# A two-layer encoder on one core: attention's weighted sum in plain float32 with two column halves of the array, in place of split operands

## The reference

```
proj = rms_norm(x) @ w_in            # latents (A), q/k/v of 6 heads (B), q/k/v of 4 heads (C)
o_a = dense attention, 6 heads       # q and k have 64 + 32 rotary features, v has 64
o_b = dilated sliding attention, 6 heads of 64
o_c = neighbourhood attention on a 16 x 64 grid, 4 heads of 64, with a bias
x = x + concat(norm(o_a), norm(o_b), norm(o_c)) @ w_out
x = x + square(relu(rms_norm(x) @ w_mlp_in)) @ w_mlp_out
```

```
p = softmax(scores)                  # scores: queries x keys
o = p @ v                            # the weighted sum: v has 64 columns per head
```

## Time and profile before

| quantity | value |
|---|---|
| median of three runs | 2985.09 us |
| span of the profiled execution | 2983.4 us |
| TensorE matmul busy | 2876.5 us (96%) |
| VectorE busy | 1733.5 us (58%) |
| ScalarE busy | 1081.0 us (36%) |
| mean granted TensorE clock | 0.983 |
| attention, layer 1 and layer 2 | about 292 to 665 us and about 1762 to 2145 us |

### The profile page before, as it was taken

How to read it: one execution, slowest core, us unless ns; L and a number is a source line. 1 busy time by engine, 2 the same in 40 slices (tenths; PEclk the granted TensorE clock), 3 DMA queues, 4 the chain that set the end, 5 groups by cost and what they waited for, 6 DMA issues and landing times.

```text
span 2983.4 us, 43794 instructions
## 1 busy us (share of the span) xinstructions
PE 2876.5 (96%) x14640; PEld 2454.8 (82%) x14640; DVE 1733.5 (58%) x3038; ACT 1081.0 (36%) x2056; POOL 26.5 (1%) x53
## 2 busy tenths in 40 slices
PE   7999999979999999999999999999799999999998
PEld 7998888867888888888799988887688888888886
DVE  5642778865555455455656337788655555455457
ACT  5332768864311111111334236777632111111113
POOL 0000000000000000000000000000000000000000
PEclk9999999989999999999999999999799999999999
DMA  5657534463111111111146573336530111111111
GB/s 192 185 179 181 123 84 94 103 160 120 43 43 56 42 42 56 42 56 49 59 166 200 168 182 88 87 93 142 133 108 29 56 42 56 42 43 55 42 61 69
DMA packets 194043, 281.45 MB, mean 94 GB/s; under 512 B 47184, under 2 KB 153296, under 8 KB 184144
## 3 DMA queue, kind: packets, MB, share of 16 engines
q1 hardware_dynamic: 190032, 262.56, 30.5%
q0 software_dynamic: 3840, 16.78, 1.5%
HBM read 208.50 MB, written 70.78 MB: 94 GB/s over the span
## 4 chain that ended last, share of the span: by engine, by line
PE 83%; DVE 5%; issue 5%; DMA 4%; ACT 2%; DVEq 1%; ACTq 0%; SPq 0%; POOLq 0%
PE ps L1349 23%; PE ps L1174 19%; PE ps L1364 17%; PE ps L1247 7%; PE ps L1264 6%; PE ps L1293 6%; DMA biasC<-in_bias_c 2%; PE ps L1304 2%; PE ps L1211 1%; PE ps L1142 1%; DVE hn L841 1%; DVE x L1095 1%; DMA values<-vst 1%; DVE vbuf L1082 1%; ACT rbuf L774 1%
## 5 line engine op out<-in xcount | busy, mean ns | idle before, releaser
L1364 PE MATMUL ps<-w_dn,hid 128*128 128x512 f32 x3072 | 713.1, 391 | 1.4
L1349 PE MATMUL ps<-hT,w_up 128*128 128x512 f32 x3072 | 702.6, 389 | 3.1 <-DVE hT L824 3.1
L1364 PEld LDWEIGHTS ps<-w_dn,hid 128*128 128x128 f32 x3072 | 573.5, 188 | 132.1 <-DVE x L1095 14.0
L1349 PEld LDWEIGHTS ps<-hT,w_up 128*128 128x128 f32 x3072 | 576.1, 188 | 123.1 <-DVE hT L824 3.6
L1174 PE MATMUL ps<-ws,hT 128*128 128x384 f32 (+3 forms) x3072 | 607.8, 356 | 6.8 <-DVE ws L824 3.5
L1174 PEld LDWEIGHTS ps<-ws,hT 128*128 128x128 f32 x3072 | 535.8, 190 | 53.6 <-issue 6.0
L1095 DVE TENSOR_TENSOR x<-ps,x 128x512 f32<-128x512 f32 x512 | 342.8, 689 | 223.8 <-PE ps L1364 223.4
L1082 DVE TENSOR_TENSOR vbuf<-rbuf 128x512 f32<-128x512 f32 x128 | 88.6, 692 | 367.5 <-ACT rbuf L774 367.5
L824 DVE TENSOR_TENSOR pT<-ps,pT 128x512 fp32r<-128x512 f32 (+1 forms) x448 | 281.6, 664 | 33.5 <-ACT pT L706 33.4
L706 ACT ACTIVATE pT<-ps 128x512 fp32r<-128x512 f32 (+1 forms) x448 | 240.2, 581 | 152.1 <-PE ps L1264 148.0
L774 ACT ACTIVATE rbuf<-ps 128x512 f32<-128x512 f32 x128 | 76.6, 598 | 550.6 <-PE ps L1349 550.6
(11 more groups left out here) (84 smaller groups left out, 2108.1 us busy)
## 6 DMA issues: line engine op xcount, KB each, us to landing
raw<-in_wstream SPq DMA_DIRECT2D x76, 1024.0 KB, 4.8
head<-feats SPq DMA_DIRECT2D x192, 256.0 KB, 5.8
feats<-tst SPq DMA_DIRECT2D x128, 192.0 KB, 2.6
values<-vst POOLq DMA_DIRECT2D x32, 384.0 KB, 3.1
head<-values SPq DMA_DIRECT2D x24, 512.0 KB, 3.9
biasC<-in_bias_c SPq DMA_DIRECT2D x16, 768.0 KB, 7.3
raw<-in_wstream SPq DMA_DIRECT2D x12, 768.0 KB, 5.7
x_park<-x SPq DMA_DIRECT2D x16, 512.0 KB, 9.1
```

Of the source, the lines that this page charges most:

```text
L1349: last = pe.matmul(ps[:, k % 2, :], w_up[0 if first else 1][:, w1, kt, ft * P:(ft + 1) * P], hT[:, w2, kt, sh * 512:(sh + 1) * 512], start ...
L1364: last = pe.matmul(ps[:, 2 + m % 4, :], hid[slot][:, w1, ft, s * P:(s + 1) * P], w_dn[1 if last_group else 0][:, w2, ft, nh * 512:(nh + 1) ...
```

## The change

The probabilities' transposes and the values are kept as plain float32, unsplit. The stationary operand of the weighted sum is now 128x64 (a key tile's values), and the output goes to PSUM partitions 0 to 63 for even key tiles and to 64 to 127 for odd ones, that is to array columns 0 to 63 and 64 to 127. The merge adds the two halves as before. For C, key groups 0 and 1 go to the low half, 2 and 3 to the high half. Each transposed group is copied once: for A and B the first group of an item by ScalarE and the second by VectorE, for C all by ScalarE. The value projections are copied once, by ScalarE. The tensor `values` holds 256 bytes per head and token, and the loads bring half the bytes in as many DMAs.

```diff
-ACT_FREES = ("a", "uq", "uk", "cqk")
+ACT_FREES = ("a", "uq", "uk", "cqk", "uv", "bv", "cv")
...
-    pT = sb("pT", [P, 2, 2, 8, 512], f32r, "H")
+    pT = sb("pT", [P, 2, 8, 512], f32, "H")
+    v_dense = [sb(f"v_dense{k}", [P, 8, HD], f32, "WS", (32 - 32 * k + 16) * KB) for k in range(2)]
+    v_grid = [sb(f"v_grid{k}", [P, 16, HD], f32, "WS", (32 - 32 * k + 16) * KB) for k in range(2)]
...
# load_values
-                            src = grid[rr:rr + 13:4, c_cols(cb):c_cols(cb) + CKC, h * P:(h + 1) * P]
-                            sp.dma_start(dst.rearrange("c (g d) -> c g d", d=P),
+                            src = grid[rr:rr + 13:4, c_cols(cb):c_cols(cb) + CKC, h * HD:(h + 1) * HD]
+                            sp.dma_start(v_grid[k][32 * rr:32 * rr + 32, 4 * cb:4 * cb + 4, :],
...
# VectorE: its half of the copies
+                        if it % 4 == 0 and b >= 2:
+                            dve.wait_ge(pv_done, l * NB + b - 1)
                         for g in ITEM_GROUPS[it]:
-                            dve.wait_ge(t_hi, l * NGR + g + 1)
...
+                            if not on_act(g):
+                                dve.wait_ge(t_done, l * NGR + g + 1)
+                                nk, k0 = group_keys(g)
+                                dve.tensor_copy(pT[:, b % 2, k0:k0 + nk, (it % 4) * P:(it % 4 + 1) * P],
...
# TensorE: weigh
-                            for w in range(2):
-                                last = pe.matmul(bank, hb[:, 4096 + kt * P:4096 + (kt + 1) * P],
-                                                 pT[:, b % 2, w, kt, :], start=(part == 0 and kt == 0 and w == 0),
-                                                 stop=(part == 3 and kt == 7 and w == 1))
+                            half = 64 * (kt % 2)
+                            last = pe.matmul(bank[half:half + 64, :], v_dense[(b // 2) % 2][:, kt, :],
+                                             pT[:, b % 2, kt, :], start=(part == 0), stop=(part == 3),
+                                             skip_group_check=True)
...
+def on_act(g):
+    it, half = GROUPS[g]
+    return ITEMS[it][0] == "C" or half == 0
```

More of the change, by code:

```diff
@@ L406, in load_values @@
                 k = n % 2
-                hb = words(head[k][:, :])
                 if n >= 2:
@@ L1258, in turns @@
                     for k, g in enumerate(ITEM_GROUPS[i]):
-                        if g >= 2:
-                            pe.wait_ge(t_lo, l * NGR + g - 1)
+                        if g >= 2 and on_act(g - 2):
+                            pe.wait_ge(pt_act, l * copies(NGR, True) + copies(g - 1, True))
+                        elif g >= 2:
+                            pe.wait_ge(pt_dve, l * copies(NGR, False) + copies(g - 1, False))
                         nk, _ = group_keys(g)
@@ L1270, in weigh @@
                     kind, h, q = ITEMS[4 * b]
-                    hb = head[(b // 2) % 2]
                     bank = ps[:, 6 + b % 2, :]
                     if part == 0:
-                        pe.wait_ge(t_lo, l * NGR + ITEM_GROUPS[4 * b + 3][-1] + 1)
+                        turned = ITEM_GROUPS[4 * b + 3][-1] + 1
+                        pe.wait_ge(pt_act, l * copies(NGR, True) + copies(turned, True))
+                        pe.wait_ge(pt_dve, l * copies(NGR, False) + copies(turned, False))
                         n, k = b // 2, b // 2 % 2
@@ L1281, in weigh @@
                     if kind == "C":
-                        c, w = part // 2, part % 2
+                        c = part // 2
                         cb = q // 2 + c
[L1284 to L1289, removed]
+                        for g, a, z in (((1, 0, 256), (2, 0, 256)), ((0, 0, 128), (3, 128, 256)))[part % 2]:
+                            half = 0 if g < 2 else 64
+                            last = pe.matmul(bank[half:half + 64, c * 256 + a:c * 256 + z],
+                                             v_grid[(b // 2) % 2][:, 4 * cb + g, :],
+                                             pT[:, b % 2, g, c * 256 + a:c * 256 + z],
+                                             start=(part % 2 == 0), stop=(part % 2 == 1), skip_group_check=True)
                     else:
                         for kt in (2 * part, 2 * part + 1):
-                            for w in range(2):
-                                last = pe.matmul(bank, hb[:, 4096 + kt * P:4096 + (kt + 1) * P],
-                                                 pT[:, b % 2, w, kt, :], start=(part == 0 and kt == 0 and w == 0),
-                                                 stop=(part == 3 and kt == 7 and w == 1))
+                            half = 64 * (kt % 2)
+                            last = pe.matmul(bank[half:half + 64, :], v_dense[(b // 2) % 2][:, kt, :],
+                                             pT[:, b % 2, kt, :], start=(part == 0), stop=(part == 3),
+                                             skip_group_check=True)
                     if part == 3:
@@ L1415, in turn_of, with copies @@
     return TURNS.index(("turn", e[1], e[2]))
+def on_act(g):
+    it, half = GROUPS[g]
+    return ITEMS[it][0] == "C" or half == 0
+def copies(n, act):
+    return sum(on_act(g) == act for g in range(n))
 def group_keys(g):
```

49 lines of the change are left out of this document (19 added, 30 removed).

## The result

The changed kernel takes 3013.67 us (median of four runs, 3012.14 to 3015.6) against 2986.94 us before. The ratio is 1.0089, with a 95% interval of 1.0076 to 1.0102: slower, as forecast, but by 27 us and not by the 103 of the forecast, and outside its range (from 3035 up). The profiled execution spans 3013.8 us.

What follows compares the result with a forecast made beforehand. TensorE's instruction stream was taken to bound kinds A and B; +98 there, +8 in kind C, 0 for bias loads and -3 at attention's start gave +103 on 2985, 3088 us; the case's own range 3045 to 3140, overall 3035 to 3210.

Steps and rivals of the forecast that it cites:

- What bounds the kernel: Attention, kinds A and B: TensorE's instruction stream sets the time; TensorE is busy 96% of the span.
- The price of a float32 product: Weighted sum: each float32 product is two records, each going through its 512 columns twice, taken as 0.44 us a record.
- Half overlap, 3T: Weighted sum, A and B: four records of T = 0.44 us take 1.32 us, as only the middle two overlap; chance 0.45.
- odd-1: Weighted sum: first record of the odd key tile's product, claimed to start beside even-2, the even product's second, not beside its first.
- even-1: Weighted sum: first record of the even key tile's product, claimed to run with nothing beside it in the other half.
- 2T: Weighted sum: four records in two fully overlapping pairs, a part at two record times plus 0.10 us; rejected in the forecast.
- The price of a change of width: Weighted sum, A and B: switching the array between whole and half width costs 0.05 us each, 0.10 a part.
- the rival to which I had given a chance of 0.10: A and B: three record times, but each width change runs the stream dry, 0.36 us, 0.72 a part; 3207 us; chance 0.10.
- The full-overlap rival: Weighted sum: both halves work side by side from the first record, width changes cost nothing; 2972 us; chance 0.20.
- Copies: Kinds A and B: VectorE falls from 2.6 to 1.9 us a step, ScalarE from 2.5 to 1.9; nothing gained.
- Kind C: Last stretch of attention: 64 parts at +0.26 us make +17, half counted as TensorE is not full: +8 us.
- Start of attention: TensorE's waits for the last value tile: subtraction goes and stores halve, half of 6.1 us gained: -3 us.

Runs made afterwards that it cites:

- the LO pass: Kernel before, LO probabilities times HI values remade as bfloat16 half-width products: kinds A and B 2974.41 us (ratio 0.9966), kind A alone 2969.35 us (0.9945).
- Wide values: Changed kernel with values stored and loaded at 512 bytes per head and token as before, the second 256 an unused ScalarE copy: 3032.19 us.

## Why the prediction was wrong

**What bounds the kernel**: right. Kinds A and B moved by what TensorE's stream moved, and VectorE's 163 us and ScalarE's 80 us less brought nothing.

**The price of a float32 product**: right. 768 records for 384 products, 0.43 us each (forecast 0.427 to 0.456), least duration 592 ns (forecast 0.60).

**Half overlap, 3T**: this is the step that failed. The prediction said that odd-1 can't lie beside even-1, "if the order of starts holds", and took the order from a trace in which nearly every record used the whole array. odd-1 starts within 0.07 us of even-1, which the prediction had named as a sign that it is wrong. Both records of the two products pair up, and 2T is what a part takes; two records hidden are worth 0.853 us, and one of them, 0.43 x 192 = 82 us, is the larger part of the 103 forecast. The Trainium skill (TensorE: Matmul & The Clock Gate, Part 3) has matmuls in program order in start and end. Across two column halves the runs don't agree: with even, even, odd, odd the second half's products ran ahead of ones written before them, at no loss. Its concurrency of column tiles they confirm, for float32 and bfloat16.

**The price of a change of width**: a price for the change stood in the sum, but it was too small for float32 halves. I took 0.10 a part from rows of full width, and it is 0.335 (full against half width in float32), not quite half of a stream run dry twice (0.72). The Trainium skill (TensorEngine Tiling (Array Packing), Key Properties) says that a change of tiling mode drains TensorE. The trace shows 0.17 us before the first load and the scores' load no longer ahead of its matmul; 192 parts pay 64 us in all. So the rival to which I had given a chance of 0.10 had the kind of cost right, but its 0.72 is further from the measured price than my 0.10. Half-width float32r in the lower half, which pays nothing, is outside that rule.

So two terms of opposite sign were off, per part: -0.43 for the overlap, +0.235 for the changes; that they partly cancel is luck. With both set right, the prediction's own sum closes: 2 x 0.43 + 0.10 + 0.335 - 1.01 = +0.285 a part, against +0.287 in A and +0.270 in B. The full-overlap rival had the columns right and the changes at nothing (2972 us); with 192 x 0.335 = 64 for them it would have been 3036, and with the 23 us that the start and kind C gave, in place of its 7, some 3020 us.

Term by term, on the profiled spans: kinds A and B +52.5 us (2 x 42 x 0.287 + 2 x 12.6 + 2 x 1.6) for a forecast of 98, kind C -13.7 for +8, the start -9.5 for -3, the rest +1.1; together 30.4.

**Copies**: right, steps with all copies on ScalarE are the same.

**Kind C**: the sign was wrong. Forecast +8 for both layers, measured -4.9 and -8.8 once the parts of kind B are taken out, together less than the 15 us that the prediction had named. Wide values took 0.7 and 5.3 of it back, in one trace, and scatter may be 4 a layer; the cause stays open. **Start of attention**: forecast -3 in all, measured -3.1 and -6.4 in the two layers; the direction was right, and the stores' halved bytes had been counted too low. Some of the 6.4 can be scatter too: the kernel before at half width, with the same code there, took 159.1 us for kind A of layer 2 where the kernel before took 162.0, and its shorter steps explain 0.4 of that.

## What to carry to other kernels

In these runs column halves of the array were worth their count of columns: with few changes of width, float32 in two halves equals split float32r at full width (2983.74 us, ratio 1.0002), no more. So a gain must come from columns that are really left out, as in the LO pass. Price a change of width and back at 0.3 us (measured: 0.335 and 0.29) for float32 and bfloat16 halves and put as many half-width products as possible behind one change, but only while the steps in between stay longer than the other engines' work in them. When a forecast rests on the order in which records start, ask whether the trace at hand has ever shown the case in which it could be different.

## What was not expected of the hardware

- Products for the two column halves start within 0.07 us of each other, and the program's order between the halves doesn't matter, at least not where two products for one half stand together (2985.4 against 2985.3 us).
- There and back between full width and half width costs 0.335 us in float32, and nothing for float32r with 64 columns in the lower half (3.388 against 3.398 us a step).
